# A hybrid decoder layer in fp32: the low parts of the weights made by GpSimd instead of VectorE

## The reference, cut to what matters

```
h = rmsnorm(x, norm_mix);  z = h @ w_in            # 1024 x 2312, columns split among the heads
att = sliding-window attention (window 128, 8 heads of 64, 2 KV heads, sinks, relative bias)
hm  = mLSTM, 4 heads (dk 64, dv 128), chunkwise, with a running-max stabiliser
x = x + [rmsnorm(att) || rmsnorm_per_head(sigmoid(o) * hm)] @ w_out      # 1024 x 1024
x = x + relu(rmsnorm(x, norm_mlp) @ w_up)**2 @ w_down                    # 1024 x 4096, 4096 x 1024
y = rmsnorm(x, norm_final)
```

## Time and profile before

| | us |
|---|---|
| median of 3 runs | 2852.89 |
| lowest, highest | 2851.8, 2856.19 |
| profiled execution, its span from first to last instruction | 2854.1 |

### The profile page before, as it was taken

How to read it: one execution, slowest core, us unless ns; L and a number is a source line. 1 busy time by engine, 2 the same in 40 slices (tenths; PEclk the granted TensorE clock), 3 DMA queues, 4 the chain that set the end, 5 groups by cost and what they waited for, 6 DMA issues and landing times. The chain is left out here.

```text
span 2854.1 us, 35133 instructions
## 1 busy us (share of the span) xinstructions
PE 2515.1 (88%) x12867; PEld 2091.4 (73%) x12867; DVE 1367.7 (48%) x2705; ACT 893.7 (31%) x1638; POOL 51.4 (2%) x87
## 2 busy tenths in 40 slices
PE   0788799999989699999989699999988787999995
PEld 0677578887777588887777588887977567888884
DVE  1356544445366544445365544446264444444442
ACT  1235333223344332223334332323333213322221
POOL 2000000000000000000000000000002000000000
PEclk9899899999999899999999899999997588999998
DMA  5221122333411122233511133233411131222221
GB/s 115 86 67 45 45 81 96 96 96 111 148 57 45 37 89 96 91 100 111 156 34 45 38 95 96 96 96 115 147 32 27 27 61 52 82 80 75 81 74 52
DMA packets 182452, 226.35 MB, mean 79 GB/s; under 512 B 22083, under 2 KB 132708, under 8 KB 182300
## 3 DMA queue, kind: packets, MB, share of 16 engines
q1 hardware_dynamic: 165596, 189.82, 21.5%
q10 hardware_dynamic: 12656, 27.30, 2.8%
q0 software_dynamic: 4064, 7.46, 1.7%
HBM read 211.57 MB, written 12.59 MB: 79 GB/s over the span
## 5 line engine op out<-in xcount | busy, mean ns | idle before, releaser
L1492 PE MATMUL ps<-a_hi,w_hi 128*128 128x512 f32 (+1 forms) x1640 | 588.2, 359 | 39.5 <-DVE a_lo L894 22.6
L1494 PE MATMUL ps<-a_hi,w_lo 128*128 128x512 f32 (+1 forms) x1640 | 589.0, 359 | 0.0
L1493 PE MATMUL ps<-a_lo,w_hi 128*128 128x512 f32 (+1 forms) x1640 | 587.9, 358 | 0.0
L559 ACT ACTIVATE w_hi<-w_raw 128x1024 fp32r<-128x1024 f32 (+2 forms) x368 | 365.0, 1032 | 652.9 <-PE ps L1494 564.6
L890 DVE TENSOR_TENSOR w_lo<-w_raw,w_hi 128x1024 fp32r<-128x1024 f32 (+2 forms) x368 | 437.8, 1199 | 264.1 <-ACT w_hi L559 220.1
L1492 PE MATMUL ps<-w_hi,u_hi 128*128 128x512 f32 (+1 forms) x1088 | 431.0, 396 | 13.0 <-DVE x L894 13.0
L1493 PE MATMUL ps<-w_lo,u_hi 128*128 128x512 f32 (+1 forms) x1088 | 427.5, 393 | 0.0
L1494 PE MATMUL ps<-w_hi,u_lo 128*128 128x512 f32 (+1 forms) x1088 | 427.1, 393 | 0.0
L1492 PEld LDWEIGHTS ps<-a_hi,w_hi 128*128 128x128 f32 x1640 | 315.5, 192 | 87.9 <-issue 29.0
L1493 PEld LDWEIGHTS ps<-a_lo,w_hi 128*128 128x128 f32 x1640 | 313.4, 191 | 44.4
L1494 PEld LDWEIGHTS ps<-a_hi,w_lo 128*128 128x128 f32 x1640 | 313.2, 191 | 42.8
(11 more groups left out here) (274 smaller groups left out, 2084.8 us busy)
## 6 DMA issues: line engine op xcount, KB each, us to landing
w_raw<-in_w_up_dram SPq DMA_DIRECT2D x128, 512.0 KB, 3.6
w_raw<-in_w_down_dram SPq DMA_DIRECT2D x128, 512.0 KB, 3.5
w_raw<-in_w_out_dram SPq DMA_DIRECT2D x32, 512.0 KB, 3.9
w_raw<-in_w_in_dram SPq DMA_DIRECT2D x24, 580.0 KB, 3.9
w_raw<-in_w_in_dram SPq DMA_DIRECT2D x24, 512.0 KB, 3.8
wide<-in_x_prompt_dram ACTq DMA_DIRECT2D x16, 512.0 KB, 4.4
x<-in_x_prompt_dram ACTq DMA_DIRECT2D x16, 512.0 KB, 5.7
w_raw<-in_w_in_dram SPq DMA_DIRECT2D x32, 256.0 KB, 2.9
```

What stands on the lines that cost most here:

```text
L559: eng.activation(w_hi[b][:, k * n:(k + 1) * n], raw[p % RAW][:, 0:n], ACT.Copy).then_inc(w_high.sem, 1)
L1492: eng.matmul(out, lh, rh, start=(k == ks[0]), stop=False)
L1493: eng.matmul(out, lh, rl, start=False, stop=False)
L1494: ins = eng.matmul(out, ll, rh, start=False, stop=(k == last))
```

## The change

GpSimd gets the subtractions. `split_vec` is gone from VectorE with all its calls; GpSimd's program gets `low_weights`, which waits for the same signal `w_high` and signals the same `w_split`, and calls it for every unit in the order of the stream, between its DMAs. The first values of `w_split` are given by GpSimd.

```
@@ gpsimd
+            def low_weights(q, u, i=0):
+                n, b = split_len(u), u % UNIT_BUFS
+                for k in range(2):
+                    p = 2 * u + k
+                    pool.wait_ge(w_high.sem, w_high.at(q, p + 1 + 16 * i))
+                    pool.tensor_tensor(w_lo[b][:, k * n:(k + 1) * n], raw[p % RAW][:, 0:n],
+                                       w_hi[b][:, k * n:(k + 1) * n].bitcast(F32), ALU.subtract).then_inc(w_split.sem, 1)
+            def low_mlp(q):
+                for u in range(U_M, U_M + 2 * len(MLP_HEAD)):
+                    low_weights(q, u)
+                u = U_M + 2 * len(MLP_HEAD)
+                with pool.Fori(0, MLP_BODY) as i:
+                    for v in range(u, u + 8):
+                        low_weights(q, v, i)
+                for v in range(u + 8 * MLP_BODY, UNITS):
+                    low_weights(q, v)
+            give_first(pool, w_split)
             pool.wait_ge(bias_sb.sem, 1)
...
             pool.memset(bias0[:, :, :], MASKED).then_inc(bias0_made.sem, 1)
+            low_weights(0, 0)
             pool.wait_ge(bias_out.sem, 16)
...
+            low_weights(0, 1)
+            with pool.Fori(0, NQ - 1) as q:
+                for u in range(2, U_M):
+                    low_weights(q, u)
+                low_mlp(q)
+                for u in range(2):
+                    low_weights(q + 1, u)
             QL = NQ - 1
+            for u in range(2, U_O + 1):
+                low_weights(QL, u)
             pool.wait_ge(pt_out.sem, pt_out.at(QL, 4 * BLK))
...
+            for u in range(U_O + 1, U_M):
+                low_weights(QL, u)
+            low_mlp(QL)
             pool.wait_ge(vec_end.sem, vec_end.at(0, 1))
@@ vector
-            def split_vec(eng, q, u, k, i=0):
-                p = 2 * u + k
-                n = split_len(u)
-                b = u % UNIT_BUFS
-                eng.wait_ge(w_high.sem, w_high.at(q, p + 1 + 16 * i))
-                eng.tensor_tensor(w_lo[b][:, k * n:(k + 1) * n], raw[p % RAW][:, 0:n],
-                                             w_hi[b][:, k * n:(k + 1) * n].bitcast(F32), ALU.subtract).then_inc(w_split.sem, 1)
...
```

More of the change, by code:

```diff
@@ L1285, in quarter @@
                 vec.n = 0
-                for u in range(1, U_T):
-                    split_vec(eng, q, u + 1, 0)
-                    split_vec(eng, q, u + 1, 1)
                 eng.wait_ge(dn_out.sem, dn_out.at(q, 0))
@@ L1299, in tm_step @@
                     ins.then_inc(tm_read.sem, 1)
[L1301 to L1305, removed]
                 def op_step(o):
@@ L1321, in op_step @@
                         tt(xs, src, xs, ALU.add).then_inc(op_read.sem, 1)
[L1322 to L1326, removed]
                 for o in range(NT):
@@ L1347, in quarter @@
                     tm_step(o + 2)
-                    tm_split(o, 3)
                     o += 3
@@ L1352, in quarter @@
                     take_values(q, NT, j)
-                tm_split(o, 4 * NT - o)
                 for o in range(o, 4 * NT):
@@ L1411, in step @@
                 def step(kind, c, half, u, i):
[L1412 to L1415, removed]
                     if u == UNITS - 4 and not last:
@@ L1440, in step @@
                                 low(l, o, t, off, w)
-                            if t == 0 and not end:
-                                split_vec(eng, nq, nu, 1, i)
                     else:
@@ L1449, in step @@
                             tt(xs, xs, ps[4 + n % 4][0:R, :], ALU.add).then_inc(dn_read.sem, 1)
-                            if n == 1 and not end:
-                                split_vec(eng, nq, nu, 1, i)
                 mlp_walk(eng, q, last, step)
-                if not last:
-                    split_vec(eng, q + 1, 1, 0)
-                    split_vec(eng, q + 1, 1, 1)
                 norm(q, tiles, 0, 2)
-            give_first(eng, w_split, dn_read, y_made, pt_vec, c_ok)
+            give_first(eng, dn_read, y_made, pt_vec, c_ok)
             for t, v in ((mp, 0.0), (Cst, 0.0), (kk, 0.0), (vv, 0.0), (rows, 0.0), (st, 1.0), (gz, 0.0)):
@@ L1469, in _ @@
             eng.wait_ge(bias0_made.sem, bias0_made.at(0, 1))
-            split_vec(eng, 0, 0, 0)
-            split_vec(eng, 0, 0, 1)
             for b in (-1, 0, 1):
@@ L1474, in _ @@
                 take_ahead(0, b)
-            split_vec(eng, 0, 1, 0)
-            split_vec(eng, 0, 1, 1)
             with eng.Fori(0, NQ - 1) as q:
```

## The result

| | before | after |
|---|---|---|
| median of the runs, us | 2854.18 (4 runs, 2851.8 to 2856.19) | 2884.64 (4 runs, 2882.03 to 2888.41) |
| profiled execution, its span, us | 2854.1 | 2886.6 |
| TensorE's mean granted clock over it | 0.933 | 0.923 |

The changed kernel is slower: the ratio is 1.0107, with a 95% interval of 1.0094 to 1.012. The forecast was 2862, the range ended at 2880. So the sign was right and the size was not: +32.5 us of span where +9.1 had been worked out, 23.4 too few.

What follows compares the result with a forecast made beforehand. TensorE was taken as the busiest engine (2515 of 2854 us), so only its waits counted. Gains of -17.3 us and a loss of +26.4 summed to +9.1, giving 2862 us, with a range of 2833 to 2880.

Steps and rivals of the forecast that it cites:

- the loss: Attention: VectorE's divisions wait for GpSimd's two pieces of T3 and of O0; 6.6 us a quarter, +26.4 in all.
- Rival 1: Both engines read SBUF freely, so divisions are not held up and only the gains stand; 2835.6 us, chance 28%.
- Rival 2: VectorE gets in between GpSimd's two pieces and keeps going; net -7.7 us, 2845 us, chance 15%.
- Rival 3: Longer idle times in attention also lower TensorE's clock; 4.6 us a quarter, +18, 2880 us, chance 12%.
- (c): Turn of a quarter and projection units F0 to F5, T0: earlier chain against slower GpSimd pieces; +0.8 us together.
- (d): T0's tiles no longer wait for VectorE's reads of PSUM behind T1's subtractions; -2.0 us.
- the credit: Turn of a quarter: raw buffer freed in time and earlier last adds bring ScalarE's chain forward; -4.0 us a quarter.
- (e): Attention blocks 1 to 3: score maxima start sooner, but only block 3's wait shrinks; -3.1 us.
- (b): End of the feed-forward, first three quarters: TensorE's wait for the last add into x shrinks; -3.3 us.
- (a): Start: the first unit's two subtractions leave VectorE's queue ahead of the first normalisation; -2.4 us.
- (f): O3's subtractions no longer stand between two tiles of the mLSTM output, ending TensorE's wait; -4.3 us.
- (g): Last quarter: VectorE no longer waits for O1's late copy, so TensorE's idle time for the x adds goes; -3.0 us.

Runs made afterwards that it cites:

- v_attn: Changed kernel with the low parts of T3 and O0 (four pieces a quarter) made by VectorE again; 2846.05 us, ratio 0.9975 to the kernel before.
- v_delay: Changed kernel with GpSimd waiting ahead of T3 and O0 until turned probabilities have been taken; 2860.7 us, ratio 1.0017 to the kernel before.
- b_read: Kernel before, with GpSimd additionally making the low parts of T3 and O0 to no use; 2897.26 us, ratio 1.0169.
- v_small: Changed kernel with GpSimd's pieces of T3 and O0 issued in four parts each; 2881.45 us, ratio 1.012 to the kernel before.
- b_late: Kernel before, with useless VectorE reads of the bias table ahead of the divisions of blocks 1 and 2, first three quarters; 2878.64 us, ratio 1.0101.
- v_proj: Changed kernel with the low parts of F2 to F5, T0 and T1 made by VectorE again; 2865.7 us, ratio 1.0043 to the kernel before.

## Why the prediction was right and wrong

**Right in kind: the loss.** "I take the upper end" held, and a little more. The divisions stand still for the whole of GpSimd's two pieces: TensorE's waits rose by 3.3 us in block 1 (5.26 less 1.99) and 4.3 in block 2 (6.28 less 1.99), 7.6 a quarter where 6.6 had been given. T3's piece is 2.64 us long, and the eight-column operation ahead of the divisions is caught too. v_attn, v_delay and b_read show the cause from three sides: other engine, other time, contention alone.

The rule cited from the Trainium skill's SBUF — State Buffer (Who interferes with whom), that a two-input or two-port instruction of VectorE waits for all of GpSimd's, is borne out by the squares, which grow, while the adds that read PSUM do not. The traces add that it holds for one GpSimd instruction at a time, not for the whole row of pieces: between two pieces one held-up VectorE operation goes ahead. Whether the rule covers the divisions is open. They read a single tile, with a column of scalars, at 0.27 us for 256 elements (2.19 us for eight); no row shows whether they were in a two-port mode, but they waited.

**Rival 1** (both read freely) is out: the waits for the divisions would have stayed at 33 us. **Rival 2** had half of the mechanism: VectorE does get in between the pieces, but for one instruction, not to "keep going". v_small shows that smaller pieces on GpSimd don't change that.

**Wrong: the sum left the clock out.** This is the step that failed most. The sum prices each wait by its own length and nothing else, so slower matmuls stand at zero in it; measured they are 16.0 of the 23.4 us that it missed. Rival 3, given 12%, was not a rival but a term. b_late shows it for T2 to T3: waits alone, 0.3 us of slower matmuls for each us of them. Rival 3's price for attention was too high, 4.6 us a quarter; in T2 to T3 it was 2.2 (6.6 / 3), from T1 to O0 it was 2.4 (9.7 / 4). That its 18 us in all come near the 16.0 is luck: 8.0 of them lie from F0 to T1, where it had none, and those 8.0 were 1.3 to 4.0 in three other kernels with the same projection. The prediction gives as its reason "I know no row that ties one wait to one drop"; that is a reason to call the term unsure, not to set it to zero.

**Wrong: step (c) and with it (d).** The costs of (c) came as worked out: in quarter 0 the losses at F2, F3, F5 and T0 were put at +3.6 and F0 to T0 grew from 53.7 to 57.5. T0's wait in quarter 1, 0.68 us before, was predicted 1.4 longer:
```profile
792.31 0.61 PE L1488 MATMUL ps<-w_hi,a_hi 128*128 128x290 f32 x1 [2.92 <-POOL w_lo L455]
```
It is 2.2 longer, since there the copies on ScalarE come close together and both pieces of 2.7 us follow each other. What failed was the credit, "that chain comes 3.2 us sooner, and 0.8 more". ScalarE in quarter 1, the norm's first operation and the first reads of zT, before (F0 starts at 726.35) and after (732.44):
```profile
730.89 1.04 ACT L581 ACTIVATE PT<-x 128x1024 f32<-128x1024 f32 x1
...
749.02 1.09 ACT L650 ACTIVATE zT<-ps 128x512 f32<-128x512 f32 x2 [13.01 <-PE ps L1494]
```
```profile
734.55 1.04 ACT L615 ACTIVATE PT<-x 128x1024 f32<-128x1024 f32 x1
...
754.17 1.08 ACT L684 ACTIVATE zT<-ps 128x512 f32<-128x512 f32 x2 [14.49 <-issue]
```
The wait for the raw piece is gone, but counted from F0 the norm starts only 2.4 us sooner (2.6 and 2.3 in the next two quarters). The rest of the 3.2 is F0's own wait, which the sum had counted already (-2.6), and the 0.8 does not show. At the reads of zT 0.9, 1.9 and 2.4 us are left: in the first two of these quarters ScalarE comes 1.3 and 0.8 us later to the loads of x that stand in between; why was not traced. So F2's wait, which the credit should have taken from 3.26 to about 0.4 in quarter 1, is still there:
```profile
758.48 0.79 PE L1488 MATMUL ps<-a_hi,w_hi 128*128 128x512 f32 x1 [3.65 <-POOL w_lo L455]
```
In the last quarter TensorE's wait for zT went from 6.34 to 4.1, by 2.2 where 3.0 had been worked out (-4.0 + 1.0). In quarters 1 and 2 the stretch from F0 to T0 grew by 2.9 and 4.1 where +0.8 had been worked out. And (d), -2.0: the wait for VectorE's reads is gone as foreseen, but T0 to T1 still became 4.6 us longer over four quarters, with T0's tiles at the slower clock. Together F0 to T1 was +1.4 in the sum and +14.6 in fact, 8.0 of it busy time. v_proj, which undoes only this, gains more than that.

**Right:** (e), block 3's wait of 3.02 us is 1.93. (b), the wait for the adds into x went from 13.0 to 9.6 us, -3.4 for the -3.3 given. F0's own wait for its low parts (0.68, 0.89 and 1.00) is gone. (a) gave -4.7 for -2.4; the sum had put the earlier loads at "nothing, up to 3 us", and no run tells whether the rest comes from them. (f) and (g) gave -9.2 for -7.3, but only 6.2 of that is waiting; 3.0 is shorter busy time, for which neither has a reason. In the feed-forward TensorE never waits for a low part of GpSimd. These gains are what the kernel with both places undone keeps.

So 13.2 us of the 23.4 that were missed are in F0 to T1, 8.0 of slower matmuls and 5.2 of waits; 13.9 are in attention, 9.7 of slower matmuls and 4.2 of waits; the other stretches came out 3.7 us better than given.

## What to carry to other kernels

Moving an elementwise operation with two on-chip inputs to an idle GpSimd is not free for VectorE: ask for each piece which VectorE instruction runs beside it and whether TensorE waits for that one, and leave those few pieces where they were. Here, 64 of 368 pieces kept on VectorE, in the projection and beside the divisions, turned a loss of 1.1% into a gain of 0.7 to 0.9%. And price a wait on a stage that already idles with the clock that it costs as well, from the granted clock of the stretch where it falls.

## What the runs showed of the hardware

- GpSimd's subtraction of two fp32 tiles took 2424 ns for 128x1024, 2692 for 128x1160 and 1288 for 128x512; VectorE's 1222, 1362 and 689.
- A VectorE instruction on a single element of 4 partitions waits as long as one on 128x256 for a GpSimd piece in flight (four of them: 5.08 us instead of 0.93).
- A reciprocal on 8 columns beside a GpSimd piece was not held up (0.20 us); a two-input operation on 8 columns was (1.35 us for 0.16).
- The two engines take turns by instruction: with four-times smaller pieces the median division took 880 ns in place of 341, and the kernel was no faster (ratio 1.012 for 1.0107).
- TensorE's granted clock fell from 0.94 to 0.83 over the stretch from T2 to T3 of quarter 1 (a mean of its levels of 1.2 and 2.4 GHz) with 7.6 to 7.7 us more of waiting, with GpSimd's work or without it; the matmuls took 0.15 to 0.35 us longer for each us of added waiting in four kernels.
- Not tried: whether it is GpSimd's reads or its write that holds VectorE up, and whether a division with a constant in place of the column of scalars would wait.
